# Expert gates of the second feed-forward: one-hot products on TensorE, or indirect accumulating transfers into device memory

## The reference, cut to what matters

```python
def peer_ffn(h, w_q, sub_keys, u_tab, v_tab):      # 8 heads, 128 x 128 experts, top 16
    q = (h @ w_q).reshape(B, S, 8, 2, 128)
    scores = jnp.einsum('bshpd,hpkd->bshpk', q, sub_keys)
    s1, i1 = lax.top_k(scores[..., 0, :], 16)
    s2, i2 = lax.top_k(scores[..., 1, :], 16)
    cand_s = s1[..., :, None] + s2[..., None, :]              # 256 candidates
    cand_id = i1[..., :, None] * 128 + i2[..., None, :]
    top_s, top_pos = lax.top_k(cand_s, 16)
    ids = take_along_axis(cand_id, top_pos)
    gate = softmax(top_s)
    ...
    act = gelu(einsum('thkd,td->thk', u_tab[ids], h))
    out = einsum('thk,thkd->td', gate * act, v_tab[ids])
```

## Time and profile before

| | |
|---|---|
| median of 3 runs | 3009.79 us (3009.45 to 3010.23) |
| the profiled execution | 3009.49 us, of which the span of the trace is 3007.7 us |
| busy share | PE 99%, PEld 89%, DVE 78%, ACT 51%, POOL 4% |
| granted TensorE clock | 0.999 of full |
| DMA | 567.88 MB, mean 189 GB/s |

### The profile page before, as it was taken

How to read it: one execution, slowest core, us unless ns; L and a number is a source line. 1 busy time by engine, 2 the same in 40 slices (tenths; PEclk the granted TensorE clock), 3 DMA queues, 4 the chain that set the end, 5 groups by cost and what they waited for, 6 DMA issues and landing times.

```text
span 3007.7 us, 53285 instructions
## 1 busy us (share of the span) xinstructions
PE 2984.1 (99%) x18836; PEld 2671.1 (89%) x18836; DVE 2345.0 (78%) x4377; ACT 1545.4 (51%) x2689; POOL 107.3 (4%) x130
## 2 busy tenths in 40 slices
PE   9999999999999999999999999999999999999998
PEld 8887887888688899899999988888799999988887
DVE  8886897887776788789899855556789889965555
ACT  5546553544654565555544445545755544444554
POOL 1010111001010000000000000000000000000000
PEclk9999999999999999999999999999999999999999
DMA  8773787876146452355544455555355544455554
GB/s 342 281 285 124 259 302 248 294 284 228 43 168 209 158 179 71 127 177 187 171 145 140 148 194 192 192 195 189 136 166 188 187 145 145 140 182 195 192 191 154
DMA packets 125268, 567.88 MB, mean 189 GB/s; under 512 B 13904, under 2 KB 14032, under 8 KB 97872
## 3 DMA queue, kind: packets, MB, share of 16 engines
q1 hardware_dynamic: 109152, 504.41, 48.7%
q0 software_dynamic: 15264, 58.73, 5.6%
q10 hardware_dynamic: 720, 3.00, 0.2%
HBM read 565.03 MB, written 1.05 MB: 188 GB/s over the span
## 4 chain that ended last, share of the span: by engine, by line
PE 89%; DVE 3%; ACT 2%; issue 0%; DMA 0%; DVEq 0%; SPq 0%; ACTq 0%
PE turn L370 47%; PE gather L370 41%; ACT arena L1601 1%; PE turn L1045 0%; ACT hT L1601 0%; ACT L1601 0%; DVE arena L2619 0%; DVE arena L2346 0%; DVE arena L2614 0%; DVE arena L2667 0%; DVE keyed L2286 0%; DVE x_rows L2348 0%; DVE arena L2634 0%; ACT expert_src_high L1601 0%; DVE arena L2283 0%
## 5 line engine op out<-in xcount | busy, mean ns | idle before, releaser
L1601 ACT ACTIVATE dense<-ring 128x1024 fp32r<-128x1024 f32 x542 | 573.7, 1059 | 372.3 <-PE gather L370 345.4
L370 PE MATMUL turn<-expert_src_high,ring_low 128*128 128x256 f32 x2600 | 724.9, 279 | 0.0
L2986 DVE TENSOR_TENSOR ring_low<-ring,dense 128x1024 fp32r<-128x1024 f32 x542 | 659.5, 1218 | 56.3 <-ACT dense L1601 53.5
L370 PE MATMUL turn<-expert_src_high,dense 128*128 128x256 f32 x2288 | 651.4, 285 | 0.3
L370 PE MATMUL turn<-expert_src_low,dense 128*128 128x256 f32 x2288 | 637.2, 279 | 0.0
L370 PE MATMUL gather<-dense 128*128 128x512 f32 x2048 | 631.9, 389 | 0.0
L370 PEld LDWEIGHTS turn<-expert_src_high,ring_low 128*128 128x128 f32 x2600 | 489.1, 188 | 0.0
L370 PE MATMUL turn<-rounded 128*128 128x512 f32 x1392 | 480.0, 390 | 0.0
L370 PEld LDWEIGHTS gather<-dense 128*128 128x128 f32 x2048 | 384.4, 188 | 80.2
L370 PEld LDWEIGHTS turn<-expert_src_high,dense 128*128 128x128 f32 x2288 | 430.5, 188 | 0.7 <-DVE ring_low L2986 0.7
L370 PEld LDWEIGHTS turn<-expert_src_low,dense 128*128 128x128 f32 x2288 | 429.6, 188 | 0.0
(11 more groups left out here) (309 smaller groups left out, 3987.5 us busy)
## 6 DMA issues: line engine op xcount, KB each, us to landing
ring<-tiles_in SPq DMA_DIRECT2D x544, 512.0 KB, 3.3
ring<-stream SPq DMA_DIRECT2D x204, 1024.0 KB, 5.5
arena<-ada_in POOLq DMA_DIRECT2D x96, 512.0 KB, 4.5
arena<-tables_in POOLq DMA_DIRECT2D x6, 1024.0 KB, 7.6
arena<-keys_in SPq DMA_DIRECT2D x2, 1024.0 KB, 8.1
arena<-c_in POOLq DMA_DIRECT2D x3, 512.0 KB, 5.6
hT<-x_in SPq DMA_DIRECT2D x2, 512.0 KB, 5.0
ring<-stream SPq DMA_DIRECT2D x2, 512.0 KB, 6.3
```

The costliest lines, as they stand in the source:

```text
L370: return nc.tensor.matmul(out, lhsT, rhs, start=start, stop=stop, skip_group_check=True)
L1601: return nc.scalar.activation(out, in_, func, **kw)
L2986: V.tensor_tensor(tile_words(t, ring_low).bitcast(R32), tile_words(t), tile_high[:, t % AHEAD, :], ALU.subtract).then_inc(S("tile_low"), 1)
```

## The change

The gates of a layer become a tensor in device memory, `gates{l}`, of 16,384 experts by 256 tokens (16.8 MB), and POOL fills it.

- **Clearing.** Sixteen stores of 1 MB of zeros for each layer are issued on SP's queue: two after every six pieces in the last eight rounds of pieces ahead of layer 0, and one after every six tiles in the last sixteen rounds of tiles of layer 0, for layer 1.
- **Choices, head by head.** `choose(h)` now does everything for one head: the two `top16`, then positions into keys for this head alone, then the offset (first key x 32768 + second key x 256 + token). Its shares add up to 12.7 low parts, 13.1 with `weigh_choices`, which normalises the previous head's gates. Before, a head had 6.3 and the block behind the heads 19. ACT takes each head's exponentials (`exponents`) after up tile 12h+4.
- **Scatter.** For each head POOL waits for `choices_ready` and for all earlier scatters to have landed, and issues 32 `indirect_dma_start` with `compute_op=add`: each adds 128 gates, one from each partition, at 128 computed places.
- **Loads.** When all are landed, POOL loads the gates of tiles 0 to 3 (128 KB each, `gate_tiles`), and each next one when DVE has used the slot (`hidden_gated`).
- **Gating.** DVE multiplies `slots[:, n, :]` by the loaded tile (`gate_hidden`), 256 columns, five tiles ahead of PE.
- **Gone:** the one-hot rows, their matmuls, `weigh`, `late_weigh`, ACT's stores, the transposes.

The diff, cut to its core:

```diff
@@ sync @@
+            def clear_gates(l, c):
+                sp.dma_start(gates_cleared[l][c], zeros.unsqueeze(1).to_broadcast([P, PIECE // T, T]))\
+                    .then_inc(S("gates_cleared"), 16)
...
+            with sp.Fori(rounds - ZERO_CHUNKS // 2, rounds) as i:
+                for s in range(SLOTS):
...
+                    if s % 3 == 2:
+                        clear_gates(0, i * 2 + (s // 3 - 2 * rounds + ZERO_CHUNKS))
...
+                    with sp.Fori(loops - ZERO_CHUNKS, loops) as i:
+                        for s in range(TILE_SLOTS):
...
+                            load_tile(t, i)
+                        clear_gates(1, i - (loops - ZERO_CHUNKS))
@@ tensor @@
-                for j in range(4):
-                    gates(j)
-                    up(BEFORE + j)
-                with pe.Fori(0, 5) as i:
-                    for j in range(12):
-                        gates(4 + j, i)
-                        up(BEFORE + 4 + j, i)
-                pe.wait_ge(S("gates_stored"), g0 + N_GROUPS)
+                with pe.Fori(0, 10) as i:
+                    for n in range(12):
+                        up(4 + n, i)
+                for n in range(124, NKEYS):
+                    up(n)
@@ scalar @@
+                def exponents(h):
+                    act.wait_ge(S("best_shifted"), 8 * l + h + 1)
+                    run(weights[:, h, :], weights[:, h, :], ACT.Exp).then_inc(S("best_exp"), 1)
                 def hidden_high(n, turns=0):
+                    act.wait_ge(S("hidden_gated"), e0 + n + 1 + 12 * turns)
...
+                for n in range(NKEYS):
+                    if n == SCORES_AT:
+                        act.wait_ge(S("choices_ready"), 8 * (l + 1))
                     early(n)
+                    if n % HEAD_TILES == 4 and n // HEAD_TILES < PEER_HEADS:
+                        exponents(n // HEAD_TILES)
+                for n in range(4):
+                    hidden_high(n)
@@ vector @@
-                    lows.share(0.63)
+                    lows.share(0.85)
...
+                    chain.add(V.tensor_tensor(match[:, :, :, :], place, steps, ALU.is_equal))
+                    lows.share(0.8)
+                    chain.wait()
+                    for j in range(2):
+                        keys = peer_idf[:, j:2 * TT:2, :].unsqueeze(2).to_broadcast([P, TT, TOPK, TOPK])
+                        of = match[:, j * TT:(j + 1) * TT, :, :]
+                        chain.add(V.tensor_tensor(of, of, keys, ALU.mult))
+                    lows.share(0.8)
+                    chain.wait()
+                    chain.add(V.tensor_reduce(chosen[:, :, :], match[:, :, :, :], AXIS.X, ALU.add))
...
+                for h in range(PEER_HEADS):
+                    choose(h)
+                weigh_choices(PEER_HEADS - 1)
+                lows.until(v0 + 2)
+
+                def gate_hidden(n, turns=0):
+                    dve.wait_ge(S("expert_gelu"), e0 + n + 1 + 12 * turns)
+                    dve.wait_ge(S(f"gates_loaded{n % GATE_SLOTS}"), 16 * ((e0 + n) // GATE_SLOTS + 1) + 48 * turns)
+                    V.tensor_tensor(slots[:, n + 12 * turns, :], slots[:, n + 12 * turns, :],
+                                    gate_tiles[:, n % GATE_SLOTS, :], ALU.mult).then_inc(S("hidden_gated"), 1)
...
                 def down(n, turns=0):
                     if n + 2 < NKEYS:
                         lows.low(v0 + n + 2, turns)
+                    if n + 5 < NKEYS:
+                        gate_hidden(n + 5, turns)
                     if n + 4 < NKEYS:
                         hidden_low(n + 4, turns)
-                gate_rows(0)
...
+                for n in range(5):
+                    gate_hidden(n)
                 for n in range(4):
                     hidden_low(n)
@@ gpsimd @@
+            def load_gates(l, n, turns=0):
+                s = n % GATE_SLOTS
+                pool.dma_start(gate_tiles[:, s, :], gates_by_tile[l][n + GATE_SLOTS * turns])\
+                    .then_inc(S(f"gates_loaded{s}"), 16)
+
+            def scatter(l, h):
+                head = PEER_HEADS * l + h
+                pool.wait_ge(S("choices_ready"), head + 1)
+                if head > 0:
+                    pool.wait_ge(S("gates_scattered"), 16 * TT * TOPK * head)
+                for c in range(TT * TOPK):
+                    pool.indirect_dma_start(
+                        gates_flat[l], bass.IndirectOffsetOnAxis(offsets[:, h, c:c + 1], 0),
+                        weights[:, h, c:c + 1], None, bounds_check=NKEYS * NKEYS * T - 1, compute_op=ALU.add)\
+                        .then_inc(S("gates_scattered"), 16)
+
+            for l in range(DEPTH):
+                pool.wait_ge(S("gates_cleared"), 16 * ZERO_CHUNKS * (l + 1))
+                for h in range(PEER_HEADS):
+                    scatter(l, h)
+                pool.wait_ge(S("gates_scattered"), 16 * TT * TOPK * PEER_HEADS * (l + 1))
+                for n in range(GATE_SLOTS):
+                    load_gates(l, n)
+                with pool.Fori(0, NKEYS // GATE_SLOTS - 1) as i:
+                    for n in range(GATE_SLOTS):
+                        pool.wait_ge(S("hidden_gated"), i * GATE_SLOTS + (NKEYS * l + n + 1))
+                        load_gates(l, GATE_SLOTS + n, i)
```

More of the change, by code:

```diff
@@ L705, in build @@
         sp_t = lr.take(10, 16)
[L708 to L725, removed]
+        peer_qT = carve(NKEYS // 2 * T - 16 * NKEYS - 16 * T, 16, T)
+        pr = Place(SCORES_AT * T, LATE)
+        peer_s = pr.take(PEER_HEADS, 2 * TT, NKEYS)
+        peer_spare = pr.take(2 * TT, NKEYS)
+        cand = peer_s.rearrange("p h (t s) k -> p h t (s k)", s=2)
+        cand_spare = peer_spare.rearrange("p (t s) k -> p t (s k)", s=2)
         def homes(name, at, n):
@@ L3072, in peer @@
-                dve.wait_ge(S("best_exp"), l + 1)
-                chain.add(V.tensor_reduce(gsum[:, :, :], best[:, :, :, :], AXIS.X, ALU.add))
-                chain.wait()
-                chain.add(V.reciprocal(gsum[:, :, :], gsum[:, :, :]))
-                chain.wait()
-                for tt in range(TT):
-                    last = V.tensor_tensor(chosen[2][:, tt, :].rearrange("p (h k) -> p h k", k=TOPK),
-                                           best[:, tt, :, :],
-                                           gsum[:, tt, :].unsqueeze(2).to_broadcast([P, 8, TOPK]), ALU.mult)
@@ new lines, in choose @@
+                    lows.share(0.8)
+                    chain.wait()
+                    chain.add(V.scalar_tensor_tensor(flat[:, :, :], chosen[:, 0:TT, :], float(NKEYS * T),
+                                                     tokens.unsqueeze(2).to_broadcast([P, TT, TOPK]),
+                                                     ALU.mult, ALU.add))
+                    lows.share(0.2)
+                    chain.wait()
+                    chain.add(V.scalar_tensor_tensor(flat[:, :, :], chosen[:, TT:2 * TT, :], float(T), flat[:, :, :],
+                                                     ALU.mult, ALU.add))
@@ new lines, in choose, with weigh_choices @@
+                    lows.share(0.2)
+                    chain.wait()
+                    chain.add(V.tensor_copy(offsets[:, h, :], flat[:, :, :].rearrange("p t k -> p (t k)")))
+                def weigh_choices(h):
+                    w = weights[:, h, :].rearrange("p (t k) -> p t k", k=TOPK)
+                    dve.wait_ge(S("best_exp"), 8 * l + h + 1)
+                    chain.add(V.tensor_reduce(gsum[:, :], w, AXIS.X, ALU.add))
+                    lows.share(0.2)
+                    chain.wait()
+                    chain.add(V.reciprocal(gsum[:, :], gsum[:, :]))
+                    lows.share(0.2)
+                    chain.wait()
+                    V.tensor_tensor(w, w, gsum[:, :].unsqueeze(2).to_broadcast([P, TT, TOPK]), ALU.mult)\
+                        .then_inc(S("choices_ready"), 1)
```

221 lines of the change are left out of this document (70 added, 151 removed).

## The result

The changed kernel takes 3398.99 us (3395.7 to 3401.25) against 3009.6 for the kernel before: a ratio of 1.129, with an interval of 1.127 to 1.131. That is 389 us slower, where 2903 was forecast, and 269 us beyond the top of the range. It is rival (a), with 256 issues of a layer at 2.20 us each in the mean, where the dearest case worked out for it had 2.0.

A forecast was written before the change was run, and what follows sets the result against it. PE, at 99% of the span, was taken as the bound: 3009.5 - 115.2 (one-hot products and transposes) + 8.6 (turn from up to down) = 2902.9, forecast 2903 us. Range 2893 to 3130, likeliest case 2895 to 2971.

The forecast's parts named there:

- rival (a): POOL's issue is the new bound; PE waits ahead of the first down tile for gate tile 0; 3131 to 3285 us; 24%.
- The path of the one-hot products: Expert up stages: 64 one-hot pieces of 0.89 us in each of two layers, and transposes, leave PE's path; minus 115.2 us.
- DVE beside the up tiles: Up stage: DVE's 31 us of work per head fits PE's 36.8 us, so it keeps up and costs nothing.
- The turn: From up to down stage: PE waits 4.3 us because the fifth gating needs slot 0 reloaded; two layers, plus 8.6 us.
- X: The end of up tile 127; slot 0's reload was to be issued at X + 0.2 and PE to start at X + 4.3.
- The down stage and the clearing: Layer 0's down stage: DVE 73%, gate loads hidden, clearing costs nothing; other end 68 us if small packets cost twice their bytes.
- The scatter: POOL's 256 indirect adds a layer, hidden within 345 us beside the up stage; ends near 1592, 63 us ahead of need.
- c: POOL's cost of one scatter issue: taken as 1.06 us, upper end 4.5; loss past 1.25, whole gain used up at 1.46.
- rival (b): Each scatter waits for its own landing: 83 us a head, 666 a layer, time 3551 us; 3%.
- The lock to the low parts: POOL's offset reads wait for DVE: half a low part, 0.61 us an issue, time 3116 us; 8 of rival (a)'s 24%.
- (c): The DMA engines are the bound: 32,768 four-byte items a layer beside tiles; at 100 ns each about 49 us a layer; 7%.
- (d): PE finds another limit in the up stage and keeps the pace of 3.7 us a tile: 3018 us; under 1%.

The follow-up runs named there:

- e_one: The changed kernel with one of the 32 scatters of each head left in (31 of 32 gates left out): 2911.79 us, ratio 0.967.
- e_turn: e_one with DVE's fifth gating moved behind the first four low parts of the hidden values: 2902.95 us, ratio 0.965.
- m_issue: A separate small program: POOL issues 24 transfers of 128 words per section beside one neighbour; an indirect add steps at 1.85 us alone, 2.52 beside two-input VectorE.
- e_half: The changed kernel with 16 of the 32 scatters of each head: 2912.61 us, one time without an interval.
- e_plain: The changed kernel with all 512 scatters as plain stores instead of adds: 3307.79 us, one time.
- m_loads: A separate kernel of transfers alone: 44 loads of 512 KB beside 40 small GpSimd transfers; 60.4 us with loads alone, 93.0 beside direct stores.

## Why the prediction was wrong

**The path of the one-hot products: right.** Up tiles stand back to back, at 2.82 us in layer 0 of the changed kernel (1700 matmuls from 1360 to 1560 us) and at 2.80 in that of e_one (1717), and the -115.2 us are there: with them, e_turn's waits of 4.6 us at the turn and 3.2 in the up stage give 2902.2, against 2902.95. That this is also the forecast 2903 is luck: there 8.6 us stood for another turn, and nothing for the up stage.

**DVE beside the up tiles: right but for 1.6 us a layer.** I had it keep up with every low part. It does, save once: the last step of head 0's shares waits 4.94 us for ACT's exponentials, which stand behind the GELU and the high part of up tile 4 in ACT's queue and behind a load of ACT's function table, and a low part is late. ACT's, DVE's and PE's lines of the changed kernel:

```profile
1311.21 1.28 ACT L1602 ACT_TABLE_LOAD   x1
1312.51 0.23 ACT L1602 ACTIVATE ring<-ring 128x32 f32<-128x32 f32 x1
...
1312.85 0.19 DVE L3059 TENSOR_REDUCE ring<-ring 128x2 f32<-128x32 f32 x1 [4.94 <-ACT ring L1602]
1312.95 1.22 DVE L2962 TENSOR_TENSOR ring_low<-ring,dense 128x1024 fp32r<-128x1024 f32 x1
...
1314.22 0.39 PE L389 MATMUL turn<-expert_src_high,dense 128*128 128x256 f32 x1 [1.59 <-DVE ring_low L2962]
```

I had worked out when the last head's choices are ready for ACT, and not how long DVE waits for the exponentials; for these I had only ACT's 0.39 + 1.05 us in a tile, without the two table loads of 1.28 us that each head's exponentials bring (74 table loads in the kernel, 52 before). By these lines the exponentials would have come 1.3 us earlier without the first of them, which is most of PE's 1.59; no run tries it. Two layers: 3.2 us.

**The turn: the mechanism right, the size half.** Predicted 4.3 us a layer, all from the reload of slot 0. In e_one it is 6.0 us of wait and 1.8 of matmuls at a granted clock of 0.61 (4.69 against the 2.88 of the earlier trace rows): 15.6 us for both layers instead of 8.6. The mis-sized term is the reload: 3.99 us from its issue and not 3.2, and the issue came at 1656.87, 1.1 us after the start of the first gating and not 0.4 (X is 1656.05 here, so X + 0.8 against X + 0.2). The slower clock I had not thought of. With 3.2 from the shares the parts give 18.8, where the sum had 8.6; e_one shows 17.4.

**The down stage and the clearing: right.** PE is not starved in layer 0's down stage. In e_one it is busy for 325 of the 325 us from 1665, with 287 GB/s and a DMA share of 0.86; the changed kernel has 271 GB/s and 0.80 in the first part. DVE is at 69% there, where 73% was forecast; e_one's whole excess is accounted for above, so the clearing's other end of 68 us isn't there.

**The scatter: the step that failed is the choice of c.** The frame was right. The window was 345 us by the prediction and 344 by the trace (first scatter at 1315.45, the up stage done at 1659.3), and the law 2 x (256c - 321) with c = 2.20 gives +484, so 3387. With 2 x 2.6 us of half clock after the hole (5.46 us for 12 matmuls against 2.88) and the 3.2 us of the shares it is 3395, against 3399 (c is read from the same trace, so this bears out the frame and not a price). What failed is the sentence "an add has two things to read for one that it writes, so I take two direct issues, 1.06 us". Measured are 1.85 us for an issue alone and 2.20 in the mean of the layer. Three parts were wrong in it:

- From the earlier trace rows I had the price of a direct issue with no add and no offsets, 0.53. m_issue gives 0.90 with the add, 1.29 with offsets and 1.85 with both. The 1.06 had no row behind it, only a reason, between ends of 0.53 and 4.5 that differ by eight times.
- The limit was c = 1.25, and the gain used up at 1.46. A value that lay within 20% of the limit, with a factor of eight between its ends, can't carry 56%. With c spread evenly by ratio between 0.53 and 4.5, 40% lies under 1.25, 47% under 1.46, and 46% over 1.7, for which I had left some 12% (15% with rival (b)).
- The lock to the low parts I had as a part of rival (a), as half a low part, 0.61 us on top of 1.06. It is up to 0.97 us for one issue (2.52 against 1.55), and in the mean over the layer (2.20 - 1.85) x 256 = 90 us and not 156 (0.61 x 256), because the second half was issued in the hole, where DVE stands still, and not every issue of the first half meets a low part. At c = 1.85 alone the time would still have been 2903 + 2 x (474 - 321) + 8 = 3217: the lock made it worse but didn't decide the sign.

A slip beside these changes nothing: at 1.06 us and heads 36.8 us apart, head 6 would have been out at 1310 + 6 x 36.8 + 36.5 = 1567, and head 7, though ready at 1555, at 1604 and not at 1592.

**The rivals.** (a) is what happened; its place (PE ahead of the first down tile, for gate tile 0) and its law hold. (b) fails: issues stand 0.30 us apart, and only between heads is a landing waited for, 2.2 to 3.7 us where I had 2.6. (c) fails: m_issue's step is 1.85 at 379 GB/s as well as alone, and the up stage ran at 2.82 us a tile with 131 scatters beside it, where the two layers of e_one have 2.80 and 2.82 (1717 and 1701 matmuls in 200 us) with 8 scatters each. (d) fails, as e_turn shows.

## What to carry to other kernels

An indirect add of 128 words holds GpSimd for 1.85 us, and for 2.52 beside a chain of VectorE subtractions of 1.26 us with two inputs in SBUF; count the issues and lay them beside the stage that is to hide them. Here it had room for some 130 (e_half's 128 end just in time), so half by the new way and half by the old one beats either. Where the sum turns on one price that no row shows, and its ends lie on both sides of the break-even, the forecast should be split by how much of the span lies on each side, whatever the reason for the middle value.

## What was not expected of the hardware

- Indirect stores without add, issued 0.30 us apart, cut TensorE to one instruction in 1.4 us after some 10 us (13 to 25 in the kernel), with no other engine at work: 130.9 us for what takes 88.7. What they share is open. Indirect adds at 1.85 us don't: 86.9. A store is cheaper for GpSimd (1.29) and dearer for the kernel (3308 us by e_plain).
- An indirect add slows beside VectorE with two inputs (1.85 to 2.52, two of its operations) and beside copies (2.18, three of them), but an indirect store (1.29) and an add without offsets (0.90) do not beside two inputs.
- Transfers of 128 adjacent words beside loads lower these from 384 GB/s to 154 (247 to 300 us of m_loads), and land after 12 us (median), where indirect stores beside loads land after 5.2. The DMA engines show as full all the while (share 1.03).
- After a gap of 6 us ahead of the down tiles the granted clock was 0.61 of full over the next 12 matmuls in the mean (that is, mostly at 1.2 and not at 2.4 GHz), and they took 1.8 us more; after one of 2.3 us it was 1.00, and they took 0.1 more.
